# Expert blocks of 128 rows against blocks of two 64-row halves with an expert each, in an encoder layer with 64 routed experts

## What is computed

```python
counts = jnp.bincount(flat_e, length=N_EXPERTS)
padded = (counts + MOE_BLOCK - 1) // MOE_BLOCK * MOE_BLOCK      # MOE_BLOCK = 128
...
def body(acc, blk):
    tok, gw, e = blk
    yb = swiglu(xt[tok], w_exp_in[e], w_exp_out[e]) * gw[:, None].astype(xt.dtype)
    return acc.at[tok].add(yb), None
```

## Time and profile before

| | us |
|---|---|
| median of 3 runs | 2883.7 (2883.22 to 2883.85) |
| span of the profiled execution | 2881.8 |
| of it, TensorE busy | 2738.3 (95%) |
| of it, GpSimd (POOL) busy | 1076.2 |
| of it, the experts from 1462.7 to 2821.0 | 1358.3 |

### The profile page before, as it was taken

The page is one execution under the profiler, slowest core; times in us unless marked ns, Lnnn a source line. Parts: engine busy times, 40 slices in busy tenths (PEclk is TensorE's granted clock), DMA queues, the critical chain, the costliest instruction groups (busy, mean ns, idle before and its releaser), DMA issues.

```text
span 2881.8 us, 31407 instructions
## 1 busy us (share of the span) xinstructions
PE 2738.3 (95%) x9145; PEld 1334.1 (46%) x9145; DVE 1581.8 (55%) x2551; ACT 691.3 (24%) x1204; POOL 1076.2 (37%) x1128
## 2 busy tenths in 40 slices
PE   7999999899999999899899999999999999999992
PEld 2345444455555455455444444444444444444440
DVE  4477356778877577778733344334343343333336
ACT  2354354366666311111100000000000000000004
POOL 2002001100000123233456656566565666556654
PEclk9999999899999999999899999999999999999996
DMA  9531010310000311311288798986978688899847
GB/s 350 182 115 55 19 33 8 128 44 12 12 12 8 136 59 59 109 60 59 76 268 233 229 324 228 315 253 166 285 220 264 183 248 248 257 306 287 244 96 255
DMA packets 189138, 464.37 MB, mean 161 GB/s; under 512 B 22524, under 2 KB 47294, under 8 KB 187646
## 3 DMA queue, kind: packets, MB, share of 16 engines
q1 hardware_dynamic: 138142, 311.89, 30.3%
q0 software_dynamic: 50912, 151.41, 21.3%
HBM read 359.28 MB, written 99.75 MB: 159 GB/s over the span
## 4 chain that ended last, share of the span: by engine, by line
PE 58%; DVE 4%; DMA 2%; issue 1%; POOL 1%; ACT 0%; DVEq 0%; SPq 0%; POOLq 0%
PE mx_pH L1263 30%; PE mx_pU L1280 15%; PE mx_pA L1901 3%; PE mx_pL L1901 3%; PE mx_pU L1963 2%; PE mx_pH L1926 2%; PE mx_pB L1934 1%; DMA s_acc<-mx_wso,ex_sidx 1%; PE mx_pB L1250 1%; DVE ring L1397 1%; DMA kT<-s_u,ex_gidx 1%; PE mx_pA L1938 0%; PE mx_pU L1911 0%; DVE mx_st L1723 0%; DMA ring<-s_acc 0%
## 5 line engine op out<-in xcount | busy, mean ns | idle before, releaser
L1263 PE MATMUL mx_pH<-ring,mx_wsi 128*128 (+1 forms) x2080 | 937.2, 593 | 6.4 <-DVE mx_h L1181 3.4
L1096 POOL DMA_INDIRECT kT<-s_u,ex_gidx x516 | 570.4, 1105 | 158.9 <-issue 153.5
L1263 PEld LDWEIGHTS mx_pH<-ring,mx_wsi 128*128 128x128 f32 x2080 | 385.4, 190 | 443.7 <-issue 443.7
L1280 PE MATMUL mx_pU<-qT,mx_hT 128*128 x1040 | 467.6, 592 | 1.5 <-DVE mx_wso L1204 1.5
L1177 DVE STREAM_TRANSPOSE mx_wsi<-kT 128x1024 f32<-128x1024 f32 x130 | 161.6, 1243 | 350.4 <-DMA kT<-s_u,ex_gidx 350.3
L1280 PEld LDWEIGHTS mx_pU<-qT,mx_hT 128*128 128x128 f32 x1040 | 197.5, 190 | 250.0 <-issue 250.0
L1120 POOL DMA_INDIRECT s_acc<-mx_wso,ex_sidx x130 | 212.2, 1632 | 189.5 <-DVE mx_wso L1204 126.7
L1204 DVE SCALAR_TENSOR_TENSOR mx_wso<-mx_pU,mx_wsi 128x1024 f32<-128x1024 f32 x130 | 166.9, 1284 | 186.5 <-PE mx_pU L1280 182.7
L1151 ACT ACTIVATE mx_hT<-mx_pB 128x256 f32<-128x256 f32 x130 | 49.8, 383 | 868.3 <-PE mx_pB L1250 868.3
L639 PE MATMUL fr_pF<-fr_uT,fr_wf 128*128 128x512 f32 x512 | 224.9, 595 | 1.3 <-ACT fr_uT L333 1.3
L1181 DVE TENSOR_TENSOR mx_h<-mx_silu,mx_pH 128x256 f32<-128x256 f32 x130 | 54.1, 416 | 305.9 <-ACT mx_silu L1141 305.6
(11 more groups left out here) (317 smaller groups left out, 3166.6 us busy)
## 6 DMA issues: line engine op xcount, KB each, us to landing
ring<-in_w_exp_in SPq DMA_DIRECT2D x64, 2048.0 KB, 13.8
qT<-in_w_exp_out SPq DMA_DIRECT2D x64, 1024.0 KB, 16.3
fr_wq<-in_w_ada SPq DMA_DIRECT2D x32, 512.0 KB, 4.9
kT<-s_u,ex_gidx POOLq DMA_INDIRECT x520
fr_wf<-in_w_in SPq DMA_DIRECT2D x16, 512.0 KB, 5.7
s_u<-v SPq DMA_DIRECT2D x16, 512.0 KB, 2.6
ring<-s_acc SPq DMA_DIRECT2D x16, 512.0 KB, 13.1
y<-ring SPq DMA_DIRECT2D x16, 512.0 KB, 6.7
```

The costliest lines, as they stand in the source:

```text
L1096: nc.gpsimd.indirect_dma_start(xg[:, u, g, :], None, u2_q, bass.IndirectOffsetOnAxis(ap=gidx[:, u, g:g + 1].bitcast(U32), axis=0)).then_in ...
L1263: m = nc.tensor.matmul(pH[:], xT[:, u, k, :], wi[:, bass.ds(slot, 1), k, :].rearrange("p a f -> p (a f)"), start=(k == 0), stop=(k == KD - 1))
L1280: m = nc.tensor.matmul(pY[:, h, :], hT[:, c, :], wo[:, bass.ds(slot, 1), c, h * 512:(h + 1) * 512].rearrange("p a d -> p (a d)"), start=(c ...
```

## The change

A block is now two halves of 64 rows, and each half has an expert of its own: an expert has as many halves as its rows need (expert 0 two at least), and halves are paired in order. The lower half (`low`) is output partitions 0 to 63 and the upper (`high`) 64 to 127, two column tiles of TensorE's array, each with its own 64 stationary columns and its own moving weights. Every matmul becomes one for each half. The lower half reads the ring; for the upper half ScalarE copies the weights of its expert out of the ring, the first ones in three parts (`IN_PARTS`) and the second ones in one. The gated rows are turned by matmuls with the identity in the same tiles, no longer by transposes of the full array. POOL scatters the two halves one after the other; a third row of `block_d` holds 16 where the two halves have different experts (and for block 0) and 0 elsewhere, POOL reads it in every block, and where it is 16 the second scatter waits until the first has landed. ScalarE reads the upper half's expert in every block. SP loads and waits for first and second weights apart, in the order: first of e, wait second of e-1, second of e, wait first of e.

```diff
+HALVES = 2
+ROWS = P // HALVES
@@ sync_part
-                load(r, w_exp_in[...], w_exp_out[...])
-                sp.wait_ge(w_in[(r - 1) % RING], q * 32 + 32)
-                sp.sem_inc(w_ready, 1)
+                load_in(r, w_exp_in[...])
+                out_place((r - 1) % RING, q + 1 if r else q)
+                load_out(r, w_exp_out[...])
+                in_place(r, q + 1)
@@ gpsimd_part
         def add(b, u, more, last=False):
-            nc.gpsimd.tensor_copy(sidx[:, u:u + 1], tok[:, bass.ds(b, 1)]).then_inc(sidx_ready, 1)
+            mixed = pool.value_load(block_d[:, bass.ds(b + 2 * P, 1)], min_val=0, max_val=16)
+            nc.gpsimd.tensor_copy(sidx[0:ROWS, u, :], tok_of[0:ROWS, :, bass.ds(b, 1)]...).then_inc(sidx_ready, 1)
...
-            nc.gpsimd.indirect_dma_start(acc_d, ..., y[:, u, :], None, compute_op=ALU.add).then_inc(scattered, 16)
+            for h, rows in enumerate((slice(0, ROWS), slice(ROWS, P))):
+                if h:
+                    pool.wait_ge(scattered, mixed + b * 32)
+                    passed(pool, apart)
+                nc.gpsimd.indirect_dma_start(acc_d, ..., y[rows, u, :], None, compute_op=ALU.add).then_inc(scattered, 16)
...
-                pool.wait_ge(scattered, b * 16 + 16)
+                pool.wait_ge(scattered, b * 32 + 32)
@@ scalar_part
         with act.Fori(0, n + 1) as t:
             for u in range(2):
                 b = t * 2 + u
+                act.reg_mov(there, expert_of(b + 2))
                 gated_rows(b)
                 silu(b + 1)
+                first_weights(kept(there))
+                act.wait_ge(y_mm, b + 2)
+                second_weights(kept(here))
+                act.reg_mov(here, kept(there))
@@ tensor_part, gated(b)
-                m = nc.tensor.transpose(pG[:, c * P:(c + 1) * P], hg[:, c * P:(c + 1) * P], ident)
+                for half in (low, high):
+                    m = nc.tensor.matmul(pG[half, c * P:(c + 1) * P], hg[:, c * P + half.start:c * P + half.stop], ident, start=True, stop=True)
@@ tensor_part, first(b, u, e)
-                m = nc.tensor.matmul(pH[:], xT[:, u, k, :], wi[:, bass.ds(slot, 1), k, :]..., start=(k == 0), stop=(k == KD - 1))
+                pe.wait_ge(in_ready, (b - 1) * len(IN_PARTS) + p + 1)
+                for k in range(k0, k1):
+                    nc.tensor.matmul(pH[low, :], xT[:, u, k, low], wi[:, bass.ds(slot, 1), k, :]..., start=(k == 0), stop=(k == KD - 1))
+                    m = nc.tensor.matmul(pH[high, :], xT[:, u, k, high], own_in(k, k + 1), start=(k == 0), stop=(k == KD - 1))
@@ tensor_part, second(b)
+            pe.wait_ge(out_ready, b + 1)
...
-                    m = nc.tensor.matmul(pY[:, h, :], hT[:, c, :], wo[:, bass.ds(slot, 1), c, ...]...)
+                    nc.tensor.matmul(pY[low, h, :], hT[:, c, low], wo[:, bass.ds(slot, 1), c, cols]...)
+                    m = nc.tensor.matmul(pY[high, h, :], hT[:, c, high], own_out[:, c, cols], ...)
@@ tables
-                step(nc.vector.tensor_scalar(nblk, pL[:, 1, 0:N_EXP], 1.0 / P, 0.5 - 0.5 / P, ALU.mult, ALU.add))
...
+                rounded_up(nblk, pL[:, 1, 0:N_EXP], ROWS, 1.0)
+                step(nc.vector.tensor_scalar(nblk[:, 0:1], nblk[:, 0:1], float(HALVES), None, ALU.max))
...
+                step(nc.vector.tensor_tensor(rows[:, 2:3], over_n[:, 1:2], over_n[:, 0:1], ALU.is_gt))
+                step(nc.vector.scalar_tensor_tensor(rows[:, 2:3], tok0[:], 0.0, rows[:, 2:3], ALU.is_equal, ALU.max))
+                step(nc.vector.tensor_scalar(rows[:, 2:3], rows[:, 2:3], 16.0, None, ALU.mult))
...
+                rounded_up(done, cum[:], HALVES, 1.0)
```

More of the change, by code:

```diff
@@ L1016, in attention, with experts @@
     nc.all_engine_barrier()
-def experts(nc, ctx, u2_d, acc_d, count_d, block_d, left, weights, cst, places_left, banks, signals, apart):
+def experts(nc, ctx, u2_d, acc_d, count_d, block_d, left, weights, cst, places_left, own, banks, signals, apart):
     FH = 2 * D_E
@@ L1026, in experts @@
     S = 32
-    wi, wo, g2, xg, raw, gidx, w_in, gathered, raw_in = left
+    wi, wo, g2, xg, raw, gidx, w_in, w_out, gathered, raw_in = left
     w_exp_in, w_exp_out = weights
@@ L1242, in tensor_part @@
         here, there = pe.alloc_register("ex_here"), pe.alloc_register("ex_there")
+        low, high = slice(0, ROWS), slice(ROWS, P)
         def kept(reg):
@@ L1407, in mixing @@
     list_d, acc_d, count_d, block_d = route
-    first_w, second_w, gates, xg, raw, gidx, w_in_exp, gathered, raw_in = left
+    first_w, second_w, gates, xg, raw, gidx, w_in_exp, w_out_exp, gathered, raw_in = left
     GQ = NQ // NKV
@@ L1812, in tables @@
                 dve.wait_ge(count_mm, 1)
[L1813 to L1819 removed]
+                nblk, cum, done = ez[:, 0, :], sg, ez[:, 1, :]
@@ new lines, in tables, with rounded_up @@
+                part, over_sum, at, rows = tb[:, 0:2], tb[:, 2:4], tb[:, 4:6], tb[:, 6:9]
+                over_n = rows[:, 0:2]
+                by_part = lambda x: x.unsqueeze(1).to_broadcast([P, HALVES, N_EXP])
+                by_expert = lambda x: x.unsqueeze(2).to_broadcast([P, HALVES, N_EXP])
+                def rounded_up(out, x, n, least):
+                    step(nc.vector.tensor_scalar(out, x, 1.0 / n, 0.5 - 0.5 / n, ALU.mult, ALU.add))
+                    step(nc.vector.tensor_scalar(out, out, float(2 ** 23), None, ALU.add))
+                    step(nc.vector.tensor_scalar(out, out, -float(2 ** 23), least, ALU.add, ALU.max))
@@ L1836, in tables @@
-                step(nc.vector.tensor_scalar(sm[:, 6:7], cum[:, N_EXP - 1:N_EXP], -3.0, None, ALU.add))
+                for c in range(HALVES):
+                    i = nc.vector.tensor_scalar(part[:, c:c + 1], tok0[:], float(HALVES), float(c), ALU.mult, ALU.add)
+                step(i)
+                over, before = junk[:, 0, 0:HALVES, :], junk[:, 1, 0:HALVES, :]
+                step(nc.vector.tensor_tensor(over, by_part(cum[:]), by_expert(part), ALU.is_le))
+                step(nc.vector.tensor_reduce(over_n, over, AX.X, ALU.add))
@@ new lines, in tables @@
+                step(nc.vector.tensor_tensor(before, over, by_part(nblk), ALU.mult))
+                step(nc.vector.tensor_reduce(over_sum, before, AX.X, ALU.add))
+                step(nc.vector.tensor_tensor(at, part, over_sum, ALU.subtract))
+                step(nc.vector.scalar_tensor_tensor(at, over_n, float(T // ROWS), at, ALU.mult, ALU.add))
+                for c in range(HALVES):
+                    i = nc.vector.tensor_scalar(at[:, c:c + 1], at[:, c:c + 1], float(N_EXP * T // ROWS + c), None, ALU.min)
```

220 lines of the change are left out of this document (120 added, 100 removed).

## The result

| | kernel before | changed kernel |
|---|---|---|
| median, us | 2883.6 (2883.2 to 2883.9) | 3114.4 (3107.4 to 3119.9) |
| span of the profiled execution | 2881.8 | 3113.0 |
| first scatter to last scatter | 1475.8 to 2830.9 = 1355.1 | 1482.6 to 3057.6 = 1575.0 |
| turn of POOL, scatter to scatter | 129 x 10.50 | 80 x 13.0, 31 mixed x 17.1 |

The changed kernel takes 1.08 times as long (95% interval 1.0784 to 1.0816): +231 us, where +80 was forecast, outside the range of 2850 to 3050. There are 224 half scatters, so 112 blocks, as counted; 31 blocks have two experts, and with block 0 there are 32 waits for a first half, of which 31 lie within the 111 turns. Of the 231 us, 220 lie between the first and the last scatter.

The account below looks back on a forecast made before the run. TensorE bounds the kernel before at 10.52 us a block; POOL would bound the changed one: 56 x 10.9 + 56 x 13.1 + 31 x 3.3 = 1446 against 1368 us, with small parts +80, so 2963.7 us, range 2850 to 3050.

Parts of the forecast that it names:

- rival B: TensorE's matmuls: half tiles do not overlap fully, 14.1 us a block, about 3097 us; chance 0.03.
- POOL's part: POOL's turns from scatter to scatter in the changed order: 1446 us against 1368, +78.
- Turn beside a load: POOL's turn while weights load: landing 9.0 + register read 2.8 + 1.3 = 13.1 us, counted 56 times.
- Quiet turn: POOL's turn with no load: issues and gathers 7.3 + register read 2.3 + 1.3 = 10.9 us, counted 56 times.
- Two issues in place of one: POOL's scatter: issuing 64 rows takes 1.05 us each, against 1.63 for 128; high bound 1.63.
- The register read: POOL, between landing and row numbers, covered by nothing: 2.3 us quiet, 2.8 beside a load (bounds 2.0 and 5.5).
- Mixed blocks: POOL: 31 blocks wait for the first half's landing, 3.3 us added each, 102 us in all.
- the low bounds: POOL's terms at their least (issue 0.82, read 2.0, half landing 3.1): 26 + 40 + 30 us off, 2868.
- On TensorE it hides behind queued matmuls: TensorE's own register read, about 2.3 us by its medians, was taken as covered.
- rival A: POOL keeps up and TensorE sets the time at 10.73 us a block: -166, 2720 us; chance 0.19.
- Rival D: TensorE's clock drops after its waits for POOL: at most 31 x 1.7 us, 3015 us; chance 0.05.
- Rival C: Weights come late in runs of experts with one or two halves: ten stalls of 8 us, 3045 us; chance 0.08.

Follow-up runs that it names:

- e16: Kernel before with every matmul as a pair of half tiles (upper half on other values) and TensorE's read of the expert from SBUF: 2910.3 us.
- e15: Changed kernel with TensorE's and ScalarE's reads from SBUF, POOL's still from DRAM: 3116.8 us.
- e14: Changed kernel with POOL's read alone from SBUF, TensorE and ScalarE reading from DRAM: 2974.8 us.
- e11: Kernel before with each block's 128 rows scattered in two DMAs of 64 rows, the second not waiting for the first: 2911.5 us.
- e12: Changed kernel with TensorE, ScalarE and POOL all reading expert and flag from the table in SBUF: 2927.3 us.
- e10: Kernel before with an unused register read from DRAM on POOL ahead of the row numbers in every block: 3133.8 us.
- e9: Kernel before with half tiles alone (upper half on other values), TensorE's read still from DRAM: 3144.6 us.
- e3: Changed kernel with a second plane for upper halves' sums, no mixed wait, no register read on POOL and one scatter of 128 rows: 3043.9 us.
- e13: Changed kernel with two planes, one scatter, no POOL read or mixed wait, and TensorE's and ScalarE's reads from SBUF: 2796.6 us.
- e7: Kernel before with TensorE's register read from DRAM made twice in each block: 3186.0 us.

## Why the prediction was off

**Right.** 112 blocks, 31 of them mixed. Half tiles overlap fully, against the Trainium skill's rule and rival B: e16's +26.7 is 130 x 0.21. ScalarE's copies are hidden (TensorE waits 2.3 us for them in all where the weights were there in time). POOL sets the changed kernel's time: e15 gains nothing, e14 gains 140.

**Mis-sized terms of POOL's part.** By the prediction's sum: 56 x 10.9 + 56 x 13.1 + 31 x 3.3 = 1446; measured 80 x 12.99 + 31 x 17.12 = 1570. These 124 us are most of the 151 by which the forecast was short. The rest is small: the span of scatters before was 1355 and not the 1368 that was subtracted, and some 15 us lie ahead of the first scatter, in the last half and in the output.

- *Turn beside a load*, 13.1 us taken, 15.1 measured on the mean of 27. The term that was too small is "landing 9.0", taken low because POOL comes later after the load's issue. The wait for the second half ends 8.4 to 9.7 us from its scatter in these turns, which is 10.2 to 12.2 from the first's and 11.1 on the mean: near the 10.3 to 11.3 of the earlier trace rows.
- *Quiet turn*, 10.9 us taken, 11.9 measured on the mean of the other 53. That the block shown above has 10.94 is luck. The read takes 2.8 us in these and not 2.3, the second half has landed 7.6 us after the first scatter and not 7.3, and row numbers and register work take 1.5 and not 1.3.
- *Two issues in place of one*: 1.05 us each taken, 1.585 on the mean measured (1.455 where POOL makes no read from DRAM, e11, e12). The row count carries almost nothing, and the value lies near the high bound, 1.63. First to second scatter is 1.86 us for 1.35.
- *The register read*: 2.3 quiet and 2.8 loaded taken, 2.7 on the mean measured, over 6.4 in the slowest twentieth. Here the size was about right. What it is worth depends on what stands behind it: 250 us for 130 reads in the kernel before (e10), 140 for 112 in the changed one (e14), where TensorE's own read takes over.
- *Mixed blocks*: 3.3 us taken, 4.1 measured, so 127 us for the 102 of the sum.

In the range, the low bounds take 40 us for a read of 2.0 us, where the prediction's own numbers give 56 x 0.3 + 56 x 0.8 = 62.

**The step that failed in kind** is the sentence "On TensorE it hides behind queued matmuls". It was read off the kernel before, where it is true, and the change halves what the queued matmuls last, from 7.2 to 3.7 us. With half tiles alone, and the read now beside the loads of weights, this costs 234 us (e9 against e16). Nothing in the sum, the rivals or the range has this. It made rival A wrong outright: with POOL as fast as before, A promised 2720, e3 gives 3044, of which 28 are the second plane's. In the changed kernel itself it holds only what e12 gains over e14, 47 us, because POOL's turn covers it.

**Rival D, the clock**, was bounded at 52 us with a chance of 0.05. TensorE is busy for 1274 of the 1575 us, where e13 needs 1189 for the same matmuls: 85 us more, at a granted clock of 0.93 on the mean against 0.99. By the intervals of the granted clock 59 of them are lost to it while TensorE is busy (65 against 6 us); the rest goes with the 119 pauses, as in e9. It is no rival to the forecast's path, since it comes with the pauses: e16, without any, has a clock of 1.00. Not every pause brings it: e11, with its 23 short waits, has 1.00 too. How much of the whole time it costs while POOL rules, no run shows.

**Rival C**, late weights: 2 waits of 14.7 us, hidden by slow blocks; it is first seen in e13, where blocks are fast.

Together: 1189 us of matmuls, 85 more with the lower clock and the broken overlap, and 301 of pauses make the 1575 us from first to last scatter, against 1355 before. 171 us of the pauses are for POOL, through the gathers, 92 behind TensorE's own read and 15 for weights.

## What to carry to other kernels

A read that hides behind queued work is covered by a number of instructions; when a change makes these shorter, or lets two run at once, ask anew whether each read, wait and register step still fits, also on engines that the change does not touch, and which transfers it now falls beside. A value that was made on the chip is better read from SBUF than from its copy in DRAM: 0.3 us against 2 to 6, and here 187 us of 3114 with no other edit. When the first bound falls and the time does not, as in e3, look at once for waits that name no other engine.

## What was not expected of the hardware

- A register read from DRAM takes two loads here, the address and the value: 1.8 to 2.0 us at the least, 2.7 to 4.8 on the mean. Without a weight load beside it it takes 2.5 us in the changed kernel, beside one 5.1, and in e7 two reads take 4.4 and 10.0. The Trainium skill (DMA: Bandwidth & Descriptors, Latency and other measured facts) gives a floor of about 600 ns for such a load; the trace agrees for the second one on GpSimd and TensorE (0.65 us at the least; ScalarE's came down to 0.46), but a whole read is never that short in these runs. The same read from SBUF is one load of 0.28 to 0.30 us and hardly varies.
- An indirect scatter of 64 rows of 4 KB with addition takes 1.455 us to issue, one of 128 rows 1.633: 89% for half of the rows.
- TensorE's sequencer begins its read from DRAM with 17 or 18 matmul records still to start, whether these are full or half tiles.
- Pairs of half tiles (64 columns of the array, 512 moving columns) take 0.43 us, as long as one full matmul.
